# State-space mixer on one core: a group of gate products moves from chunk 2 to chunk 3, and the gate evictions behind the last exponential

## The reference

```python
xbc = jax.nn.silu(xbc + conv_b)
xs, bm, cm = jnp.split(xbc, [...], axis=-1)
a_cs = jnp.cumsum(da, axis=2)
seg = a_cs[:, :, :, None, :] - a_cs[:, :, None, :, :]
decay_in = jnp.exp(jnp.where(causal, seg, -jnp.inf))
cb = jnp.einsum('bclgn,bcsgn->bclsg', cc, bc)
y_diag = jnp.einsum('bclsgj,bcsgjp->bclgjp', cb[..., None] * decay_in, xdt)
# the state goes from chunk to chunk: dec * state + st, y_off = cc @ prev * exp(a_cs)
y = (y_diag + y_off) + x_heads * d_skip
y = y.reshape(b, s, GROUP_WIDTH) * jax.nn.silu(z)        # z is the gate
y = rmsnorm(y, norm_g)                                   # in two groups of 256
```

## Time and profile before

| | |
|---|---|
| median of 3 runs | 2953.86 us (2947.92 to 2956.01) |
| profiled execution | 2957.77 us, span 2956.0 us |
| PE busy | 97% of the span |
| DVE busy | 54% |
| ACT busy | 37% |
| mean granted clock of PE | 0.991 |
| chunk loop of `ssd()`, layer 0 and layer 1 | from 472.66 and from 1006.28 us of the span |

### The profile page before, as it was taken

The page is one execution under the profiler, slowest core; times in us unless marked ns, Lnnn a source line. Parts: engine busy times, 40 slices in busy tenths (PEclk is TensorE's granted clock), DMA queues, the critical chain, the costliest instruction groups (busy, mean ns, idle before and its releaser), DMA issues.

```text
span 2956.0 us, 34145 instructions
## 1 busy us (share of the span) xinstructions
PE 2860.3 (97%) x14401; PEld 2381.9 (81%) x14401; DVE 1590.1 (54%) x2184; ACT 1092.9 (37%) x1409; POOL 118.8 (4%) x123
## 2 busy tenths in 40 slices
PE   7999998899999989999999999999999999999998
PEld 7878887888888878888876888888888886788886
DVE  4355347734535665553556574625746364656455
ACT  4322443432234233332545433325323354543332
POOL 0020000001000000000100000000000010000000
PEclk9999999899999999999999999999999999999999
DMA  5242222223221223543521243423534341224342
GB/s 204 75 138 72 72 72 81 95 79 103 83 86 53 76 80 114 144 113 117 114 100 39 97 136 128 128 100 114 144 114 131 112 102 58 86 100 143 108 134 86
DMA packets 67816, 305.19 MB, mean 103 GB/s; under 512 B 6916, under 2 KB 7106, under 8 KB 40016
## 3 DMA queue, kind: packets, MB, share of 16 engines
q1 hardware_dynamic: 53216, 263.21, 26.0%
q0 software_dynamic: 12992, 32.00, 5.6%
q10 hardware_dynamic: 1456, 7.80, 0.9%
HBM read 294.60 MB, written 2.10 MB: 100 GB/s over the span
## 4 chain that ended last, share of the span: by engine, by line
PE 84%; DVE 8%; ACT 3%; DMA 3%; issue 2%; ACTq 0%; SPq 0%; DVEq 0%
PE G L483 14%; PE G L485 14%; PE G L484 14%; PE G L495 8%; PE G L497 8%; PE G L496 8%; PE G L959 3%; PE G L961 3%; PE G L960 3%; DMA raw<-in_stream 2%; DVE w_lo L1697 2%; ACT w_hi L1120 1%; PE A L1010 1%; PE A L1032 1%; PE A L672 1%
## 5 line engine op out<-in xcount | busy, mean ns | idle before, releaser
L483 PE MATMUL G<-xT_hi,w_hi 128*128 128x512 f32 (+1 forms) x2368 | 881.6, 372 | 7.1 <-DVE xT_lo L1752 4.3
L485 PE MATMUL G<-xT_hi,w_lo 128*128 128x512 f32 (+1 forms) x2368 | 870.9, 368 | 0.0
L484 PE MATMUL G<-xT_lo,w_hi 128*128 128x512 f32 (+1 forms) x2368 | 870.5, 368 | 0.0
L1697 DVE TENSOR_TENSOR w_lo<-raw,w_hi 128x2048 fp32r<-128x2048 f32 (+1 forms) x215 | 491.6, 2286 | 505.4 <-ACT w_hi L1120 505.1
L1120 ACT ACTIVATE w_hi<-raw 128x2048 fp32r<-128x2048 f32 (+1 forms) x215 | 407.6, 1896 | 699.7 <-PE G L485 371.6
L483 PEld LDWEIGHTS G<-xT_hi,w_hi 128*128 128x128 f32 x2368 | 450.4, 190 | 79.2 <-DVE xT_lo L1752 5.1
L485 PEld LDWEIGHTS G<-xT_hi,w_lo 128*128 128x128 f32 x2368 | 449.9, 190 | 72.9
L484 PEld LDWEIGHTS G<-xT_lo,w_hi 128*128 128x128 f32 x2368 | 450.5, 190 | 69.0
L495 PE MATMUL G<-w_hi,xT_hi 128*128 128x512 f32 (+1 forms) x512 | 194.1, 379 | 8.7 <-issue 3.4
L497 PE MATMUL G<-w_hi,xT_lo 128*128 128x512 f32 (+1 forms) x512 | 186.8, 365 | 0.0
L496 PE MATMUL G<-w_lo,xT_hi 128*128 128x512 f32 (+1 forms) x512 | 186.6, 364 | 0.0
(11 more groups left out here) (320 smaller groups left out, 3664.6 us busy)
## 6 DMA issues: line engine op xcount, KB each, us to landing
raw<-in_stream SPq DMA_DIRECT2D x208, 1024.0 KB, 4.9
raw<-in_stream SPq DMA_DIRECT2D x80, 512.0 KB, 5.5
raw<-in_stream POOLq DMA_DIRECT2D x32, 512.0 KB, 9.4
lnr<-in_ln_rows POOLq DMA_DIRECT2D x6, 1024.0 KB, 4.9
row<-in_rows POOLq DMA_DIRECT2D x6, 512.0 KB, 6.8
x<-in_x ACTq DMA_DIRECT2D x1, 2048.0 KB, 17.6
tB<-fA ACTq DMA_DIRECT2D x4, 512.0 KB, 5.4
xn<-fB ACTq DMA_DIRECT2D x4, 512.0 KB, 8.4
```

What stands on the lines that cost most here:

```text
L483: mm(o, a, hi[:, c, at:at + n], start=start and own_start, stop=False, **k)
L484: mm(o, a, lo[:, c, at:at + n], start=False, stop=False, **k)
L485: return mm(o, wl[:, col:col + P], hi[:, c, at:at + n], start=False, stop=stop, **k)
L1697: tt(w_lo[:, s, 0:nk, :], raw[:, r, 0:nk, :], w_hi[:, s, 0:nk, :].bitcast(F32), ALU.subtract).then_inc(lo_done, 1)
```

## The change

One of PE's eight gate steps moves from chunk 2 to chunk 3. On ACT the exponential of chunk 3 stands ahead of `gate_out` and of the split. On DVE the split of chunk 3 stands behind L2137, with the wait for all gate evictions ahead of it; in layer 1 the three gate multiplications and the scaling of the sums of squares go there as well. Nothing else differs: the same instructions are issued.

```diff
--- before.py
+++ after.py
@@ -839,7 +839,7 @@
                         last = mm(A[:, 2, g * P:g * P + P], fB[:, g, c * P:c * P + P], fB[:, 2 + g, c * P:c * P + P],
                                   start=True, stop=True)
                     last.then_inc(S["d_bc"], 1)
-                    advance(gate, (2, 2, 2, 0)[c])
+                    advance(gate, (2, 2, 1, 1)[c])
                     pe.wait_ge(S["d_sub"], so_far(l, "d_sub") + c + 1)
                     if c:
                         for g in range(2):
@@ -1335,6 +1335,8 @@
                 for c in range(TILES):
                     if c == 1:
                         split()
+                    act.wait_ge(S["d_t"], so_far(l, "d_t") + c + 1)
+                    fn(sB[:, 0:1024], sB[:, 0:1024], ACT.Exp).then_inc(S["d_e"], 1)
                     if c == 3:
                         gate_out(2 if Pos.l + 1 < DEPTH else 1)
                         act.preload_act_table_set(LN_EXP)
@@ -1345,8 +1347,6 @@
                                 act.wait_ge(S["d_gm"], k // 2 + 1)
                                 fn(tA[:, k // 2, v], mix[:, k // 2, v], ACT.Square,
                                    accum_out=rs_v[:, k:k + 1]).then_inc(S["d_gs"], 1)
-                    act.wait_ge(S["d_t"], so_far(l, "d_t") + c + 1)
-                    fn(sB[:, 0:1024], sB[:, 0:1024], ACT.Exp).then_inc(S["d_e"], 1)
 
             act.preload_act_table_set(LN_EXP)
             act.wait_ge(landed["mem0_in"], 16)
@@ -2113,23 +2113,12 @@
                         split()
                     if c == 3:
                         next_unit(2 if more else 1)
-                        if not more:
-                            results_read()
-                            for k in range(3):
-                                tt(mix[:, k, :], mix[:, k, :], tB[:, k, :], ALU.mult).then_inc(S["d_gm"], 1)
                     t = sB[:, 0:1024].rearrange("p (h n) -> p h n", n=P)
                     dve.wait_ge(S["d_bc"], so_far(l, "d_bc") + c + 1)
                     tt(t, A[:, 0:2, :].rearrange("p b (h n) -> p (b h) n", n=P),
                        heads(small[:, 4, 8 * c:8 * c + 8], 8), ALU.subtract).then_inc(S["d_sub"], 1)
                     dve.wait_ge(S["d_sub"], so_far(l, "d_sub") + c + 1)
                     tt(t, t, c1v("upto_neg").unsqueeze(1).to_broadcast([P, 8, P]), ALU.min).then_inc(S["d_t"], 1)
-                    if c == 3:
-                        split()
-                        if more:
-                            results_read()
-                        else:
-                            dve.wait_ge(S["d_gs"], 6)
-                            ts(rs_v[:, 0:6], rs_v[:, 0:6], 1.0 / 256, EPS, ALU.mult, ALU.add).then_inc(S["rs_in"], 1)
                     dve.wait_ge(S["d_e"], so_far(l, "d_e") + c + 1)
                     if c:
                         dve.wait_ge(S["d_y"], so_far(l, "d_y") + c)
@@ -2138,6 +2127,15 @@
                                  sB[:, g * 512:g * 512 + 512].rearrange("p (h n) -> p h n", n=P),
                                  A[:, 2, g * P:g * P + P].unsqueeze(1).to_broadcast([P, 4, P]), ALU.mult)
                     ins.then_inc(S["d_sc"], 1)
+                    if c == 3:
+                        results_read()
+                        if not more:
+                            for k in range(3):
+                                tt(mix[:, k, :], mix[:, k, :], tB[:, k, :], ALU.mult).then_inc(S["d_gm"], 1)
+                        split()
+                        if not more:
+                            dve.wait_ge(S["d_gs"], 6)
+                            ts(rs_v[:, 0:6], rs_v[:, 0:6], 1.0 / 256, EPS, ALU.mult, ALU.add).then_inc(S["rs_in"], 1)
                     m, part = mix[:, c, :], sB[:, 0:512]
                     dve.wait_ge(S["d_kv"], so_far(l, "d_kv") + c + 1)
                     dve.wait_ge(S["d_skip"], so_far(l, "d_skip") + c + 1)
```

## The result

The change makes the kernel slower by 9.1 us: 2959.61 us (median of 7 runs, 2955.21 to 2965.14) against 2950.54 us (7 runs, 2947.08 to 2956.24), ratio 1.003 with a 95% interval of 1.002 to 1.004. The profiled execution took 2964.8 us, its span is 2963.0 us.

What follows compares the result with a forecast made beforehand. With PE 97% busy, DVE's order of work from chunk 3 on was taken to set the time. +4.48 us (layer 0) and +2.49 (layer 1), clock zero, gave +7.0 on 2953.9: 2960.9 us, range 2955 to 2967.

Steps and rivals of the forecast that it cites:

- the sum: Both layers' chunk loops: +4.48 us in layer 0 and +2.49 in layer 1, +7.0 us in total; chance 0.71.
- rival A: Behind the pause in both layers: the clock returns later, slow stretches grow 3.5 us each; total +10.5 us, chance 0.21.
- Part 1, the moved group: Chunk 2 into chunk 3: moving the gate step's 12 matmuls makes chunk 3 start 1.92 us earlier in each layer.
- PE's wait of about 0.9 us in chunk 2: Before chunk 2's L857: PE waits near 0.9 us for DVE L2137, so not all of 2.72 us is won.
- Part 2, the wait for ACT's chain: Behind chunk 3's exponential: DVE waits for ACT's evictions and split; net +4.48 us in layer 0, +2.49 in layer 1.
- The gain of 1.6 us from the moved multiplications in layer 1: Layer 1, chunk 3: three L2119 multiplications moved behind L2122 get out of PE's way, winning 1.6 us.
- Part 3, the clock behind the pause: GEMMs behind the pauses: half-clock stretches stay about 5.8 us (layer 0) and 5.0 us (layer 1), so zero change.
- Part 4, what costs nothing: SP queue's load waits some 6 us in layer 0, POOL's memory-row load issues 2.7 us earlier; neither costs time.
- Rival B: Chunk 3's start: something other than L2146's chain holds PE, so 2 x 1.92 us are missing; 2964.7 us, chance 0.04.
- Rival C: Behind the loop: xn and the gated mix are not PE's wait; 10.8 us less, 2943.1 us, chance 0.04.
- Signs named ahead: Profile after: no DVE wait before chunk 2's L2146, chunk 3's L857 near 1.9 us, PE idle 11 and 8 us before L672.
- the two signs of being wrong: DVE not standing before its last split; half-clock matmuls behind the pauses lasting clearly more or less than 5 to 6 us.

Runs made afterwards that it cites:

- e4_fine: The change with gate steps cut in four, 3 more of the last step's 12 matmuls staying in chunk 2; ratio 1.0019 against before.
- r1_fine: Second profile of e4_fine, the same kernel unchanged; one run, 2955.0 us.
- e2_order_only: The change with PE's gate steps of before, so only the new order on ACT and DVE; ratio 1.0042 against before.
- e3_mend: The change's layer 0 with ACT's memory-row squares and root first, DVE's split behind xn, gated squares later; layer 1 as e5_holes; ratio 0.9987 against before.
- e6_warm_after: The change plus matmuls nobody reads behind chunk 3's L857 (76 in layer 0, 50 in layer 1); ratio 1.0022 against before.
- e9_mend_warm: e3_mend plus unread matmuls before chunk 3's L857 in layer 1 and behind the memory-row transposes in layer 0; 2939.16 us, ratio 0.9964 against before.
- e1_pe_only: Before with only PE's gate step moved from chunk 2 to chunk 3, ACT and DVE order kept; ratio 1.0011 against before.
- e5_holes: Before with DVE reordered: gated squares (layer 0) or two gate multiplications (layer 1) in chunk 2's wait, layer 0's other squares later; ratio 0.9986.
- e7_warm_before: Before plus unread matmuls in PE's chunk 3 pauses, before L857 and, in layer 0, behind it and behind the memory-row transposes; ratio 0.9981.

## Why the prediction was right, and where it was not

- **The range and the direction held** (2955 to 2967, and "somewhat slower, about what can be told from no change"). The size was 2 us short: +9.1 against +7.0. That 2960.9 lies only 1.3 us from the measured 2959.6 is luck: the starting point was 3.3 us too high and the step 2.1 us too small. The medians alone also can't tell the sum from rival A's +10.5, since both lie in the interval of 5.9 to 11.8 us; what follows rests on the distances.
- **Part 1, the moved group.** PE's wait of about 0.9 us in chunk 2 was 0.77, and L2144 came without a wait; L836 of chunk 3 started 7.18 us behind chunk 2's difference, 9.11 before: 1.93 us earlier, 1.92 forecast. The step that failed is the next one, "L836, L839 and DVE L2122 of chunk 3 all come 1.92 us earlier": L836 ran at half clock, and the difference of chunk 3 came at 11.31 in place of 11.61 us behind that of chunk 2, only 0.30 us earlier. The missing term is a dip of the clock inside chunk 3, 1.62 us in each layer (11.31 against 9.69 in e4_fine). Without it the sum is right to 0.1 us in both layers, as e4_fine and r1_fine show (+4.57, +2.62).
- **Part 2, the wait for ACT's chain.** 6.60 us of ACT's chain to 0.01; e2_order_only measures the order alone at +6.48 and +4.53 us, where the forecast's terms give 6.40 and 4.41. The gain of 1.6 us from the moved multiplications in layer 1 is 1.53 there (chunk 3's difference 11.60 behind chunk 2's, 13.13 before). That PE's need stands behind this wait is shown from the other side by e3_mend.
- **Part 3, the clock behind the pause.** "The same stretches, so zero" was off in layer 0: 2.9 us at half clock in place of 5.8, which gave back 1.2 us between GEMM and last transposes; in layer 1 it was right (+0.07). So the dip's 3.2 us stand against 1.2 given back, and the net is the 2 us by which I was short. The forecast came near because two misses of the clock had opposite signs.
- **Part 4, what costs nothing.** Nothing else shows up between the two places: from the last transposes of layer 0 to chunk 2's difference of layer 1 are 482.4 us before and 483.3 with the change, and the change's stretch at half clock from 581.0 lies in between.
- **Rival A** (the slow stretches behind the pause grow by 3.5 us) did not happen: 2.9 and 5.2 us. The clock did cost more, but at another place, ahead of the pause.
- **Rival B** (chunk 2's gain isn't there) named the right 1.9 us, nearly lost to the dip, for a wrong reason: L836 did start on L2156's release.
- **Rival C** (the tail is not what PE waits for) is refuted by the 10.71 us before L672.
- **Signs named ahead**: of those for the profile after, all were there but one. L857 of chunk 3 was to take 1.9 us and took 2.25 and 2.49, the clock falling during it. Of the two signs of being wrong, the second came in layer 0: the matmuls at half clock behind the pause last 2.9 us, clearly less than 5 to 6. The clock is the part of the forecast that failed, before the pause and behind it.

What makes the dip stays open. It appears only where chunk 2 has the hole: in layer 0 in 5 of 7 profiles with one step and the hole before L857, which are 4 of 5 kernels (the change twice, e6_warm_after, e3_mend, e9_mend_warm), in neither of the 2 of the kernel with the hole filled, and in none of the 5 kernels with two steps. But both profiles of e1_pe_only have the hole, with the same pauses to 0.02 us, and no dip. A rival stands that no run tests alone: when in time the same stretch falls. Chunk 2's difference of layer 0 is at 494.9 to 495.0 or 496.4 us in the profiles with the dip, at 495.4 in e1_pe_only and at 495.6 and 495.7 in e4_fine and r1_fine, so filling the hole also moved the stretch next to where it had no dip even with the hole. In layer 1 the dip is there at 1034.5 and not at 1030.3 (e1_pe_only) or 1033.8 and 1034.0 (filled). The hole is thus a condition that fits all profiles with a dip, and not shown to be the cause. The dips themselves, and their price of 1.6 us, are the same in both profiles of the change.

## What to carry to other kernels

Before an engine's work is moved to where another is idle, read what stands behind it in the list of every engine that waits for it. Here ACT's 6.6 us of evictions and table loads lay free of charge beside a chunk; put behind the last exponential they stood, by DVE's waits for them, ahead of all that PE needed behind the loop. Look at the clock ahead of a pause as well as behind it: in four of the five kernels with a new pause of 0.8 us a stretch at half clock followed, for a cause that isn't settled. In a stretch that one engine's chain bounds, take work off that chain into its holes (e5_holes), up to where it begins to wait for another engine, and fill PE's pauses if its clock matters (e7_warm_before).

## What the runs showed of the hardware

- The granted clock fell while PE was working, not only while it stood: in the change it goes from 1.00 to 0.50 at 502.6, inside L836, after pauses of only 0.77 and 0.24 us around L857, and is at full again from 506.0. The Trainium skill, page "TensorE: Matmul & The Clock Gate", section "Why this matters for your kernels", speaks of long idle gaps. Here five profiles have the fall with no pause longer than 0.8 us in chunk 2, and two profiles with the same pauses don't have it.
- Matmuls whose result nobody reads, issued in pauses of some 2 to 3.6 us, brought 5.6 us (e7_warm_before, ratio 0.9981, interval 3 to 8 us), and both GEMMs behind them ran at full clock from the first matmul. Issued only ahead of the transposes of layer 0, with 3.14 us of idle time behind those, they left the GEMM starting at half clock (e6_warm_after).
